# Splitting each attention step of an interleaved transformer kernel into two plan steps

## What is computed

```python
for l in range(DEPTH):                                   # 2 layers
    aq, ak, av, bq, bk, bv, iq, ik, iw, cq, ck, cg, cv, cgate = mixer_inputs(rmsnorm(x, norm1[l]), w_in[l], ...)
    oa = diff_attend(aq, ak, av, mask, lam)              # 6 heads; two softmax maps, subtracted
    ob = dsa_attend(bq, iq, iw, bk, bv, ik, mask, 256)   # 5 heads; only the 256 best keys of an indexer
    sc, oc = hgrn2(cq, ck, cg, cv)                       # 5 heads; gated linear recurrence
    x = x + merge_heads(oa, ob, oc, ...) @ w_out[l]
    x = x + conv_ffn(rmsnorm(x, norm2[l]), ...)          # up, causal conv of width 3, silu * gate, down

def diff_attend(q, k, v, mask, lam):
    p = softmax(where(mask, q @ k.T * DA ** -0.5, NEG_BIG))
    return (p[:, :, 0] - lam * p[:, :, 1]) @ v
```

## Time and profile before

| | |
|---|---|
| median of 3 runs | 4133.53 us (4132.4 to 4150.61) |
| the profiled execution | 4136.72 us, of which the span is 4134.9 us |
| PE busy, its weight loads | 93%, 73% |
| DVE, ACT, POOL busy | 54%, 27%, 16% |
| mean granted TensorE clock | 0.965 |

### The profile page before, as it was taken

How to read it: one execution, slowest core, us unless ns; L and a number is a source line. 1 busy time by engine, 2 the same in 40 slices (tenths; PEclk the granted TensorE clock), 3 DMA queues, 4 the chain that set the end, 5 groups by cost and what they waited for, 6 DMA issues and landing times. The chain is left out here.

```text
span 4134.9 us, 54316 instructions
## 1 busy us (share of the span) xinstructions
PE 3826.3 (93%) x21836; PEld 3035.8 (73%) x21836; DVE 2217.6 (54%) x4505; ACT 1121.7 (27%) x2666; POOL 648.4 (16%) x732
## 2 busy tenths in 40 slices
PE   7977889999999999999899989999889999799997
PEld 6755677777776767777667777887667777588886
DVE  1753555599944554549455544589835465421112
ACT  1123333211134342321333232111144433211111
POOL 2200211301001042120000015311000101421013
PEclk9988999999999999999999999999999999899999
DMA  4332223412122123342221213332211211332223
GB/s 139 92 92 66 68 78 97 137 55 68 54 84 69 49 84 94 92 126 76 74 91 49 64 60 111 121 118 89 69 55 54 74 41 61 105 116 79 65 76 92
DMA packets 149475, 339.53 MB, mean 82 GB/s; under 512 B 30104, under 2 KB 64472, under 8 KB 135912
## 3 DMA queue, kind: packets, MB, share of 16 engines
q1 hardware_dynamic: 89448, 291.04, 22.4%
q10 hardware_dynamic: 59776, 45.02, 3.8%
HBM read 299.33 MB, written 36.68 MB: 81 GB/s over the span
## 5 line engine op out<-in xcount | busy, mean ns | idle before, releaser
L710 PE MATMUL PS<-xn,wring 128*128 128x272 f32 (+1 forms) x8448 | 1980.9, 395 | 60.7 <-ACT dense L1005 29.3
L710 PEld LDWEIGHTS PS<-xn,wring 128*128 128x128 f32 x8448 | 1628.6, 195 | 366.5 <-issue 42.9
L710 PE MATMUL PS<-dense,wring 128*128 128x256 f32 (+1 forms) x2816 | 665.1, 394 | 23.1 <-ACT res L974 12.5
L1559 POOL TENSOR_TENSOR xT<-xT,res 128x272 f32<-128x272 f32 (+1 forms) x320 | 254.0, 795 | 2693.0 <-ACT res L974 2632.2
L710 PEld LDWEIGHTS PS<-dense,wring 128*128 128x128 f32 x2816 | 538.8, 194 | 124.9 <-issue 20.3
L1344 DVE MAX8 top<-scr 128x8 f32<-128x384 f32 (+6 forms) x418 | 367.5, 879 | 12.5
L1345 DVE MATCH_REPLACE8 scr<-top,scr 128x384 f32<-128x384 f32 (+6 forms) x418 | 359.9, 861 | 0.0
L974 ACT ACTIVATE res<-PS 128x272 f32<-128x272 f32 (+1 forms) x320 | 123.1, 389 | 596.8 <-PE PS L710 568.2
L718 PE MATMUL PS<-wring,xn 128*128 128x256 f32 (+1 forms) x1152 | 266.3, 390 | 2.0 <-ACT dense L988 1.3
L718 PEld LDWEIGHTS PS<-wring,xn 128*128 128x128 f32 (+1 forms) x1152 | 212.3, 186 | 48.9 <-issue 6.9
L710 PE MATMUL PS<-catT,wring 128*128 128x272 f32 (+1 forms) x1024 | 234.5, 390 | 8.9 <-DMA wring<-in_wo 8.4
(11 more groups left out here) (165 smaller groups left out, 3323.2 us busy)
## 6 DMA issues: line engine op xcount, KB each, us to landing
wring<-in_wu SPq DMA_DIRECT2D x88, 1024.0 KB, 4.9
wring<-in_wf SPq DMA_DIRECT2D x88, 512.0 KB, 3.9
wring<-in_wo SPq DMA_DIRECT2D x64, 512.0 KB, 3.6
wring<-in_wd SPq DMA_DIRECT2D x96, 320.0 KB, 2.9
wring<-in_wd SPq DMA_DIRECT2D x64, 384.0 KB, 3.1
wring<-in_wn SPq DMA_DIRECT2D x16, 1024.0 KB, 5.1
kv<-out_projT ACTq DMA_DIRECT2D x48, 256.0 KB, 3.2
out_projT<-dense SPq DMA_DIRECT2D x40, 272.0 KB
```

What stands on the lines that cost most here:

```text
L710: mm = nc.tensor.matmul(PS[:, dbank(t.g0), 0:cw], wtile(t.q, i), rhs, start=(kk == a), stop=(kk == b - 1))
L1559: nc.gpsimd.tensor_tensor(x, x, res[:, i % NRES, 0:cw], ALU.add).then_inc(s_res, 1)
```

## The change

Each item step of B becomes two steps of the plan on all three engines. PE yields between everything else and the second turning; ACT yields after copies(s-2, 0), and does copies(s-2, 1) and expo(s) in the second step; DVE does all its work in the first. `step_times` gives each half half the nominal time, and `step_groups` the same group twice. So B has 117 steps where it had 59 (even m), and 95 where it had 48 (odd m). No instruction of a mixer or a turn is added or removed.

```diff
             if it.g == "b":
-                out.append((3.5 * k + 0.2, 0.5 + 2.1 * k, 0.6 + 2 * k, 0))
+                one = 3.5 * k + 0.2, 0.5 + 2.1 * k, 0.6 + 2 * k, 0
             else:
-                out.append((5 * k + 0.3, 0.9 + 3.2 * k, 1.3 + 4.6 * k, 0))
-        return out + [(1, 1, 0, 0)] * 3
+                one = 5 * k + 0.3, 0.9 + 3.2 * k, 1.3 + 4.6 * k, 0
+            out += [tuple(x / 2 for x in one)] * 2
+        return out + [(0.5, 0.5, 0, 0)] * 6
...
-        out.append(g)
+        out += [g, g]
...
                 if s >= 3 and m % 2 == 0:
                     values(s - 3)
+                yield
                 if 2 <= s < len(items) + 2:
                     turned(s - 2, 1)
                 yield
...
                 if 2 <= s < len(items) + 2:
                     copies(s - 2, 0)
+                yield
+                if 2 <= s < len(items) + 2:
                     copies(s - 2, 1)
                 if s < len(items):
                     expo(s)
...
                     combine(s - 1)
+                yield
                 yield
```

## The result

The change is slower by 0.73%: 4169.09 us, the median of 5 runs (4158.52 to 4178.21), against 4138.09 us (4132.4 to 4150.76) for the kernel before. The ratio is 1.0073, with a 95% interval of 1.0051 to 1.0095, about 31 us. The forecast of 4148 us was 21 us too low. The time lies inside the range of 4120 to 4174, near its upper end, but outside the forecast's own 4136 to 4160. By the prediction's bound of 20.7 us it is slower, to which it gave 0.34, and not the same, to which it gave 0.56.

The account below looks back on a forecast made before the run. PE, busy 3826.3 of 4134.9 us, bounds the kernel, with DVE pacing the searches. Terms -3.3 + 5.6 + 17.3 + 0 - 5 = +14.6 us on the 4133.5 median gave 4148 us; range 4120 to 4174.

Parts of the forecast that it names:

- C: Searches: 8 dense turns leave for attention, though DVE mostly sets the pace there; +17.3 us, bounds 0 to +30.
- A: Attention: changed cover of PE's waits for copies of bank 4 after turnings; -3.3 us, bounds -19 to +8.3.
- B: Attention: exponentials on ACT wait behind a dense turn's eviction, delaying scores of group a; +5.6 us, bounds 0 to +16.
- E: Attention, mixers 0 and 2: new turns partly fill PE's holes; -5 us, bounds 0 to -11.
- D: Recurrences: they lose 5 turns, where PE waits for single short chains; 0, with 5 us on either side.
- searches paced by DVE throughout: Searches: all 8 turns that leave make holes of full length, +30 us; 4166 us in all; chance 0.33.
- PE is the pace after all: Searches: DVE's lead of about two turns each is real, so leaving turns cost 0; 4131 us; chance 0.16.
- the clock in m = 0: Mixer 0: three more turns lift the granted clock from 0.83 and 0.90, saving 31 us; 4117 us; chance 0.09.

Follow-up runs that it names:

- weights alone: The kernel before with whole steps, each 0.3 us heavier in the plan, so turns lie nearly as in the change; 4135.26 us, ratio 0.9995.
- split alone: The change with half steps 0.15 us lighter each, so each phase has nearly as many turns as before; 4164.71 us, ratio 1.0065.
- ACT late: The change with PE's yield behind both turnings, while ACT does the second copy and exponentials in the second half; 4176.49 us, ratio 1.0098.

## Why the prediction fell short, point by point

The range held, but the account behind it lacked the main cost of the change: what came out is an error of some 30 us, partly covered by another of 14 us the other way. That it stayed inside the range is in part luck.

The traces can be cut at the first product of the indexer, the first scores and the last values of each mixer. All three kernels below have the same turns in each part: B got 13.75 more, X 7.5 fewer, the rest 6.25 fewer than before (matmuls of dense turns divided by 16; the ends of the parts fall a little otherwise than the plan's 13, 8 and 5). At 3.83 us a turn that is +52.7, -28.7 and -23.9 us. What is measured beyond it is what the other things cost:

| us against before | X | B | rest |
|---|---|---|---|
| weights alone, measured | -14.5 | +30.2 | -24.0 |
| beyond its turns | +14.2 | -22.5 | -0.1 |
| the change, measured | -18.2 | +73.9 | -14.2 |
| beyond its turns | +10.5 | +21.2 | +9.7 |
| the change, group b combined first, measured | -13.6 | +35.2 | -20.7 |
| beyond its turns | +15.1 | -17.5 | +3.2 |
| forecast beyond turns | +17.3 (C) | -2.7 (A, B, E) | 0 (D) |

**C was right in its sum, not in its parts.** Turns that leave the searches leave holes. X of m = 3, before and with the weights alone, in this order:

```profile
2621.00:2985.00 364.00, 343.78 (x1489) 280.65 (x1488) 330.79 (x506) 54.80 (x125) 59.67 (x68) 0.97 0.30 96
```

```profile
2620.00:2980.00 360.00, 336.20 (x1465) 274.91 (x1464) 331.28 (x506) 54.00 (x123) 58.38 (x66) 0.97 0.31 96
```

PE does 7.6 us less and the search ends only 4 us sooner, with DVE as busy as before. Over the four searches 14.2 us stay behind, for 17.3 forecast. By mixer they are about -0.4, +9.0, +4.0 and +1.7 us, where the forecast had 3.8, 2.7, 5.4 and 5.4: two turns left m = 0 for nothing, and m = 1 lost more than their length, in part by clock (0.99 to 0.97). That the sum fits is luck as well. The sign it named isn't there: PE's waits behind evictions in X of m = 3 were to grow from 14.4 to some 20 us and are 13.4, or 12.7 in the change; what grew is one wait for a norm on DVE, from 3.4 to 8.4 us. The rival "searches paced by DVE throughout" wanted 30; "PE is the pace after all" wanted 0 and is wrong here, though by time alone the 0.9995 of this kernel (0.9984 to 1.0006) can't be told from the -5 us that E without C would give. Its "about two turns each" is also misread for m = 2, where a lead of 3.9 us is one turn.

**E was too small.** With -22.5 us in place of -5, attention takes in the moved turns at far less than their length. It is the reason that C isn't seen in the time of that kernel. The size is rough: this trace is 8.3 us shorter than that of before, where the medians differ by some 2. B of m = 2, before and with the weights alone:

```profile
1990.00:2276.00 286.00, 267.59 (x1465) 198.83 (x1463) 137.64 (x462) 106.36 (x343) 22.15 (x29) 0.99 0.21 65
```

```profile
1985.00:2275.00 290.00, 278.45 (x1528) 208.68 (x1527) 138.71 (x464) 108.29 (x349) 22.92 (x31) 1.00 0.23 69
```

PE does 10.9 us more in 4 us more. Over the four B, PE's idle time falls by 12.2 us, and (1 - clock) x time by about 11, from 52.1 to 41.0 by the clocks as printed, to two digits. The second part is what the rival "the clock in m = 0" looked for, but in m = 0 itself it gave 4.9 of the 31 us. By mixer the -22.5 are -7.0, +4.0, -11.7 and -7.8 us, where the forecast had -4, 0, -1 and 0: it looked at the waits of turnings for DVE in m = 0 and passed over m = 2 and m = 3. B of m = 0 was to grow by less than 11 us: it grew by 8.3 with the weights alone and by 12.8 in the change.

**A was right in sign and about in size.** Turnings and values behind copies were 49.7 us together and are 43.9: -5.8, forecast -3.3. The forecast put the first near 30 (26.0) and the second over 10 (17.9). Two things it didn't have are mixed in: one wait of 5.70 us behind a store (last section), and turnings that wait for `combine` now and so no longer for a copy. With group b's order turned both before and after, the sum goes from 57.3 to 53.5 us, -3.8.

**B was right in sign; its size depends on the plan.** Scores behind exponentials are 16.0 us, and 10.1 with the weights alone at the same turns: +5.9, forecast 5.6. Against the kernel before it is +1.3. With the turns as before they are 27.9 for 14.7, +13.2, inside the bounds of 0 to 16. All of the 16.0 lies in m = 0 and m = 2 (11.0 and 5.0); the 3 us that the forecast had for the odd mixers are nowhere.

**D was right** within its 5 us with the weights alone (-0.1; it is -6.6 after the attention of m = 1 and +8.1 after that of m = 2, and -3.8 lie before the first search, where the programs don't differ). In the change the rest shows +9.7. Of these 9.8 us between the two, 5.1 lie before the first search and 3.6 after the last values, where the programs don't differ. That is scatter between executions; the profiled one of the change was 9 us over its median, that of the weights alone 7 us under.

**The step that failed is a term that isn't in the sum.** The part on A counts what stands between a turning and its copy on ACT. It never asks who else waits for a turning. The second turning also frees the buffer for `maxima` of group b, and DVE has `combine` queued behind that. The prediction names that rule for ACT, under B ("ACT never passes a waiting instruction"), and didn't apply it to DVE. B against the weights alone, with the same turns: 43.7 us more, and 5.0 more once the order on DVE is turned. B of m = 1 with the weights alone, of the change, and of the change with group b combined first:

```profile
1157.00:1562.00 405.00, 381.55 (x2065) 283.03 (x2065) 190.71 (x438) 163.81 (x352) 65.56 (x74) 0.98 0.20 62
```

```profile
1163.00:1585.00 422.00, 389.02 (x2066) 287.99 (x2066) 193.82 (x438) 157.11 (x352) 67.58 (x74) 0.96 0.20 59
```

```profile
1154.00:1559.00 405.00, 380.00 (x2063) 283.14 (x2064) 193.87 (x433) 156.20 (x352) 67.59 (x74) 0.98 0.20 62
```

The same matmuls to within three: 17 us longer in the change, 9.5 us of it idle and 7.5 us the same work at a lower clock, and back again. So the waits alone don't make up the term: in the two odd mixers those for `combine` of group b grow by 13.2 us, from 5.2 to 18.4, and fall to 0 with the order turned. The rest of what the order gives back is other idle time, the clock, and some scatter between executions. By the ratios the split costs 1.0073 - 0.9995 = 0.78%, 32 us, where A and B had 2.3: the missing term is some 30 us. The split alone, at 0.65%, gives some 25. Against it stands that C and E together were put at +12.3 and came to -2 us (0.9995), and the kernel before was at 4138.1 and not at 4133.5 in the five runs: 30 - 14 + 4.6 = 20, the 21 us that the forecast was too low.

**What stays open.** Why the split of group a in the odd mixers alone costs 0.33% and that of group b alone 0.25%, and both 0.91%. With group b's order turned, all yields of the odd mixers together cost 0.22%, so whatever group a adds is small once `combine` isn't late. The rows show that the split of group a alone adds 5.5 us to the waits for `combine` of group b (15.9 to 21.4); that the rest of its 0.33% acts through them too is argued, not shown. No run separates the clock's share from that of the waits.

## What to carry to other kernels

When an instruction is moved later, list every semaphore that it raises and follow each one: not only who takes its result, but who may write the buffer that it reads, and what is queued behind that waiter on an in-order engine. Of two instructions on one queue, put the one whose inputs are ready ahead of the one that waits for a buffer, and do it for each kind of work apart: here it was worth 0.84% in group b, and doing it in group a as well gave 0.5% of it back. Turns moved out of a phase must be priced at both ends: 14 us of holes in the searches were paid for by 22 us in attention.

## What the runs showed of the chip

**Idle time of PE often brought slower matmuls with it, but not at a fixed rate.** Between the change and the same kernel with `combine` of group b first, 16.5 us of idle PE and 24.1 us of busy PE go, with the same matmuls. Against the kernel before, in idle and busy us, the change has +20.6 and +20.9, the split alone +17.6 and +11.8, the odd mixers alone +21.2 and +15.9, ACT late +26.8 and +20.7, and `combine` first in both groups +9.9 and -2.1. After the 2.42 us at 1203.91 the granted clock of the next 20 us is 0.84. It takes no wait of 2.4 us: with ACT late a dense turn at 1207.39 takes 5.52 us as well, behind waits of 1.02 and 0.89 us. Idle share alone doesn't explain it: in the kernel before, the stretch of 1225 to 1245 has PE busy for 16.03 of 20 us and a clock of 1.00, and in the change it is busy for 15.96 us (with 90 matmuls for 93) and has 0.84. What decides was not isolated.

**A copy can wait for a store to memory.** Evictions of projections wait on ACT until an earlier store has left their buffer, and whatever is queued behind them waits too. In B of m = 1 of the change:

```profile
1575.93 0.40 ACT L984 ACTIVATE dense<-PS 128x272 f32<-128x272 f32 x1 [8.23 <-DMA out_projT<-dense]
1576.22 0.48 ACT L1121 ACTIVATE scr<-PS 128x384 f32<-128x384 f32 x1
1576.76 3.25 PE L829 MATMUL PS<-scr,kv 128*64 128x128 f32 x14 [5.70 <-ACT scr L1121]
```

An eviction put in front of the second copy carried an 8.23 us wait for a DMA into attention; PE stood for 5.70 us. It is half of the 11.2 us of this line in the change, and with `combine` of group b first it is still there (longest 5.3).
